# Attention of a one-core kernel with two accumulator banks and four score banks instead of one and five, values ahead of scores on TensorE, and its first loads in parts and in another order

## The reference, cut to what matters

```python
def chunk_mask(qpos, kpos):
    return (kpos // CHUNK)[None, :] <= (qpos // CHUNK)[:, None]          # CHUNK = 64

def mla_block_attend(qn, qp, kn, kp, v, qpos, kpos):
    s = jnp.einsum('bqhd,bkhd->bhqk', qn, kn) + jnp.einsum('bqhr,bkr->bhqk', qp, kp)
    s = jnp.where(chunk_mask(qpos, kpos), s.astype(F32) * MLA_SCALE, NEG_INF)
    p = jax.nn.softmax(s, axis=-1).astype(v.dtype)
    return jnp.einsum('bhqk,bkhd->bqhd', p, v)

def mla_prompt(q_nope, q_pe, ckv, kpe, w_ukv, pos):
    kv = jnp.einsum('bsl,lhe->bshe', ckv, w_ukv)
    k_nope, v = kv[..., :MLA_NOPE], kv[..., MLA_NOPE:]
    ...      # query block i attends to keys 0 .. (i + 1) * 128
```

## Time and profile before

| what | us |
|---|---|
| median of 3 runs (lowest, highest) | 3573.41 (3569.66, 3576.82) |
| the profiled execution | 3574.15, of which its span 3572.2 |
| PE busy, weight loads | 3074.6 (86%), 2356.9 (66%) |
| DVE busy | 1547.0 (43%) |
| ACT busy | 1063.8 (30%) |
| `mixer` | 0 to 1497.7 |
| `attention` | 1497.7 to about 2253 |
| the other blocks | to 3572.2 |

### The profile page before, as it was taken

How to read it: one execution, slowest core, us unless ns; L and a number is a source line. 1 busy time by engine, 2 the same in 40 slices (tenths; PEclk the granted TensorE clock), 3 DMA queues, 4 the chain that set the end, 5 groups by cost and what they waited for, 6 DMA issues and landing times. The chain is left out here.

```text
span 3572.2 us, 78385 instructions
## 1 busy us (share of the span) xinstructions
PE 3074.6 (86%) x28855; PEld 2356.9 (66%) x28856; DVE 1547.0 (43%) x3462; ACT 1063.8 (30%) x2645; POOL 436.1 (12%) x716
## 2 busy tenths in 40 slices
PE   5999999999999998588898989699719999999980
PEld 5888888888888887455555555355417776776660
DVE  0455555555555556377686868232310000000007
ACT  1333333333333333143444434122102222222220
POOL 0000000000000000100000000011142232222220
PEclk9999999999999999699999999899859999999995
DMA  4000010000011110200000010433227897774336
GB/s 171 26 25 25 25 28 25 25 25 26 26 29 32 28 30 23 59 9 22 16 16 22 1 33 1 148 126 129 86 103 240 265 346 237 240 216 88 76 65 217
DMA packets 136050, 297.30 MB, mean 83 GB/s; under 512 B 29403, under 2 KB 87037, under 8 KB 121341
## 3 DMA queue, kind: packets, MB, share of 16 engines
q1 hardware_dynamic: 113629, 215.65, 17.8%
q0 software_dynamic: 19520, 67.15, 8.1%
q10 hardware_dynamic: 2592, 9.96, 0.7%
HBM read 208.19 MB, written 84.53 MB: 82 GB/s over the span
## 5 line engine op out<-in xcount | busy, mean ns | idle before, releaser
L700 PE MATMUL mx_bank<-mx_xT,mx_w_in 128*128 128x128 f32 x5168 | 648.7, 283 | 23.7 <-DMA mx_w_in<-in_w_in 23.2
L700 PEld LDWEIGHTS mx_bank<-mx_xT,mx_w_in 128*128 128x128 f32 x5168 | 607.4, 195 | 78.8 <-issue 69.6
L1396 PE MATMUL at_bank<-at_kT,at_qT 128*128 128x512 f32 (+5 forms) x656 | 296.5, 539 | 2.4 <-DVE at_vals L1520 2.4
L2184 DVE SCALAR_TENSOR_TENSOR ex_th<-ex_th,ex_bank 128x256 f32<-128x256 f32 x64 | 27.0, 422 | 580.6 <-ACT ex_th L2100 580.6
L1368 ACT ACTIVATE at_PQ<-at_bank,at_nms 128x512 f32<-128x512 f32 (+5 forms) x328 | 193.1, 596 | 278.4 <-DVE at_nms L1496 183.2
L2171 PE MATMUL ex_bank<-ex_wd,ex_hT 128*128 x512 | 234.4, 601 | 2.1 <-ACT ex_hT L2106 2.1
L2151 PE MATMUL ex_bank<-ex_wg,ex_xT 128*128 x1024 | 233.9, 382 | 1.5 <-SPq L2021 1.5
L2151 PEld LDWEIGHTS ex_bank<-ex_wg,ex_xT 128*128 128x128 f32 x1024 | 196.1, 192 | 55.5 <-issue 31.6
L2151 PE MATMUL ex_bank<-ex_wu,ex_xT 128*128 x1024 | 231.5, 379 | 0.0
L1427 PEld LDWEIGHTS at_bank<-at_PT,at_vals 128*64 128x64 f32 (+1 forms) x2208 | 119.3, 139 | 156.3 <-issue 82.4
L1539 DVE COPY at_PT<-at_bank 128x512 f32<-128x512 f32 (+3 forms) x328 | 196.8, 601 | 56.8 <-PE at_bank L1408 42.8
(11 more groups left out here) (315 smaller groups left out, 4892.4 us busy)
## 6 DMA issues: line engine op xcount, KB each, us to landing
ex_wg<-in_w_eg SPq DMA_DIRECT2D x32, 1024.0 KB
ex_wu<-in_w_eu SPq DMA_DIRECT2D x32, 1024.0 KB
ex_wd<-in_w_ed SPq DMA_DIRECT2D x32, 1024.0 KB
mx_x<-in_x SPq DMA_DIRECT2D x19, 512.0 KB, 4.5
ro_x<-in_x SPq DMA_DIRECT2D x17, 512.0 KB, 3.9
scr_hx<-ro_h SPq DMA_DIRECT2D x17, 512.0 KB, 2.7
scr_acc<-ro_ha SPq DMA_DIRECT2D x17, 512.0 KB, 3.0
co_r<-scr_acc SPq DMA_DIRECT2D x17, 512.0 KB, 3.7
```

Of the source, the lines that this page charges most:

```text
L700: ins = pe.matmul(dst, w_in[:, k, col:col + n], xT[:, k, :], start=(k == 0), stop=(k == KC - 1))
L1396: t.mark(pe.matmul(bank[n % SB][:, 0:wd], qT[h][keys(h), j * P:(j + 1) * P], kT[h][keys(h), k0 * P:k0 * P + wd], start=True, stop=True), f ...
```

## The change

Three things. **Banks:** `SB` goes from 5 to 4, so scores use banks 0 to 3 and transposes 4 and 5; rows of even j accumulate their values in bank 6, odd ones in bank 7, each with its transposed reciprocals beside it. **Order and plan:** on PE a step is now values, `row_rec`, scores n + 4, transposes n; `row_rec` comes one step after the row's last values (`turned`), and ACT's copy and DVE's output with it; the first values of row j wait for output j - 2. The plan of value blocks comes out the same but for the last steps of a turn (84: three blocks instead of one; 86: none instead of two). **Loads:** SP first waits for PE's signal, which PE now gives after POOL's memsets alone; then it issues the weights, the prompt's latents in four parts, each with its own semaphore, and the rest. PE waits for a part before the K group that reads it, and for rotary keys and identity only before the first scores.

```diff
-    AHEAD, SB, TB = 4, 5, 2
+    AHEAD, SB, TB = 4, 4, 2
...
-        step = max(step, place[j, 1, g] + LAG, free)
+        step = max(step, place[j, 1, g] + LAG, free.get(j - 2, 0))
...
         if i + 1 == len(pairs) or pairs[i + 1][0] != j:
+            while step in row_end:
+                step += 1
+            if step not in share:
+                share[step] = 0
             row_end[step] = j
-            free = step + 2
+            turned[step + 1] = j
+            free[j] = step + 3
...
+        def summed(j):
+            return bank[6 + j % 2][:, 0:P]
+
+        def turned_sum(j):
+            return bank[6 + j % 2][:, P:2 * P]
...
-            sp.dma_start(lat[:, :, 0:n], lt[:, :, 0:n]).then_inc(latents.sem, 16)
...
+            def first_loads():
+                for k in range(4):
+                    cols = slice(512 * k, 512 * k + 512)
+                    sp.dma_start(lat[:, :, cols], lt[:, :, cols]).then_inc(lat_in[k], 16)
...
+                if isinstance(t.i, int):
+                    first_loads()
                 t.w0(ten, last_scores)
...
         def _(pe):
-            pe.wait_ge(latents.sem, latents.done(0))
             pe.wait_ge(setup, 6)
...
                         if gi == 0:
-                            if j > 0:
-                                t.w(vec, f"out_{j - 1}")
+                            if j > 1:
+                                t.w(vec, f"out_{j - 2}")
...
+                    pe.wait_ge(lat_in[n], 16 if n < 4 else 32)
                     for c in range(CKV):
...
+                pe.wait_ge(latents.sem, latents.done(0))
                 t.arrived(q_in)
...
                 for n in range(steps):
+                    for _ in range(share.get(n, 0)):
+                        next(v)
+                    if n in turned:
+                        row_rec(t, turned[n])
                     if n + AHEAD < count:
                         scores(t, n + AHEAD)
-                    for _ in range(share.get(n, 0)):
-                        next(v)
-                    if n in row_end:
-                        row_rec(t, row_end[n])
                     if n < count:
                         transposes(t, n)
```

More of the change, by code:

```diff
@@ L1196, in attention, with in_order @@
         if i + 1 == len(pairs) or pairs[i + 1][0] != j:
+            while step in row_end:
+                step += 1
+            if step not in share:
+                share[step] = 0
             row_end[step] = j
-            free = step + 2
-    steps = max(max(share) + 1, count)
+            turned[step + 1] = j
+            free[j] = step + 3
+    steps = max(max(share) + 2, count)
     last_use = {n: max(m for m in range(count) if m % NP == n % NP) for n in range(NP)}
-    def in_order(ahead, before, at, after):
+    def in_order(ahead, before, at, after, scores_last=False):
         names = [x for n in range(min(AHEAD, count)) for x in ahead(n)]
         for n in range(steps):
-            names += ahead(n + AHEAD) if n + AHEAD < count else []
-            names += before(n) + (at(n) if n < count else []) + after(n)
+            later = ahead(n + AHEAD) if n + AHEAD < count else []
+            names += before(n) + later if scores_last else later + before(n)
+            names += (at(n) if n < count else []) + after(n)
         return names
@@ L1217, in pv_names @@
                 out.append(f"PV{j}_{g}")
[L1218 removed]
+        return out + ([f"recT{turned[n]}"] if n in turned else [])
     def max_names(n):
@@ L1268, in attention @@
             ("tensor", ten_names), ("vector", vec_names), ("scalar", act_names), ("gpsimd", pol_names)))
-        latents = Dmas(nc, ctx, "at_latents", 10)
+        latents = Dmas(nc, ctx, "at_latents", 7)
+        lat_in = [ctx.enter_context(nc.semaphore(f"at_lat_in{k}")) for k in range(5)]
         setup = ctx.enter_context(nc.semaphore("at_setup"))
@@ L1380, in turn @@
                             t.w0(vec, last_out)
-                        t.mark(a.activation(recb[:], bank[7][:, P:2 * P], ACT.Copy), f"rec{j}")
+                        t.mark(a.activation(recb[:], turned_sum(j), ACT.Copy), f"rec{j}")
             engine_loop(a, act, turns, turn)
@@ L1426, in values @@
                             for h, m in ((0, m0), (1, m1)):
-                                ins = pe.matmul(bank[7][64 * h:64 * h + 64, 0:P], vals[0:rows, k0 + s, 64 * h:64 * h + 64],
+                                ins = pe.matmul(summed(j)[64 * h:64 * h + 64], vals[0:rows, k0 + s, 64 * h:64 * h + 64],
                                                 PT[0:rows, m % NPT, s, :], start=(gi == 0 and s == 0), stop=end)
@@ L1513, in output @@
                     t.left(o_out)
-                t.mark(v.tensor_tensor(o_sb[:, j, :], bank[7][:, 0:P], recb[:], ALU.mult), f"out_{j}")
+                t.mark(v.tensor_tensor(o_sb[:, j, :], summed(j), recb[:], ALU.mult), f"out_{j}")
             def turn(t):
```

36 lines of the change are left out of this document (18 added, 18 removed).

## The result

The changed kernel takes **3617.03 us** (median of 4 runs, 3614.94 to 3619.21) against 3574.53 (4 runs, 3569.66 to 3576.82): the ratio is **1.0118, interval 1.0106 to 1.013**, 42.5 us slower. The forecast was 3593.5 us, 19.4 us slower. The sign held and the time lies within the wide range of the prediction (3566 to 3620 us), but it is outside the forecast's own band (3583 to 3605 us), and the loss is more than twice the one forecast. The profiled execution took 3616.22 us with a span of 3614.1 us, 41.9 us more than the span before.

A forecast was written before the change was run, and what follows sets the result against it. PE and DVE were taken as close together, neither with slack for the other's waits. Heads +37.2, second accumulator -18.8, loads -5.8 and clock +6.8 made +19.4 us on 3574.15: 3593.5 us, band 3583 to 3605, range 3566 to 3620.

The forecast's parts named there:

- Heads: Four-chunk heads, rows 12 to 15: scores n+4 wait for exp n; seven loops a turn, +9.3 us a turn, +37.2 in all.
- Loop 64 to 68: Row 14's first head, end of exp 64 to end of exp 68: 9.30 us after the change, 8.06 before.
- 68 to 72: Row 14's second head, exp 68 to exp 72: 8.92 us after the change, 7.51 before.
- the heads are cheap: Rival: DVE's waits for transposes at heads take in most delay, 0.35 us a loop left; 3559 us, faster, chance 0.15.
- The clock: PE idle at the new heads drops the clock at some: one full price a turn, +6.8 us, bounds 0 and +24.
- clock at many heads: Rival: the clock falls at half of the heads or more, +24 instead of +6.8; 3611 us, chance 0.15.
- Second accumulator: Values of row j no longer wait for output j-1: -4.7 us a turn, -18.8 us, bounds -8 and -24.
- the count said no loss: Rows 8 to 11, three chunks a head: maximum n+4 can start 2.07 us after the scaled maximum, within 2.2 us.
- Loads: Weights first, latents in quarters: first matmul at 1507.5 instead of 1513.35 us, -5.8 us once, bounds -3 and -7.
- No change: Rival: about 0.9 us a loop at the heads and no fall of the clock; 3574 us, chance 0.13.
- faster: Rival case that heads are cheap, below 0.88 us a loop: 3559 us, chance 0.15.
- Not as it says: Rival: split loads queue behind one another, first matmul where it was; 3599 us, chance 0.07 with the rest as forecast.

## Why the prediction was right in sign and wrong in size

**Heads: right.** +9.3 us a turn forecast, +9.7 measured without falls of the clock (38.9 us instead of 37.2). Loop 64 to 68 read 9.69 (9.30 forecast), 68 to 72 8.71 (8.92). That it is the bank is shown by the kernel with four banks, which loses more there, and by the one with five and two accumulators, which has 57.0 us for chunks 48 to 76 instead of 64.35. The worked loop was short by 0.4 us, in the time from scores to transposes. The rival "the heads are cheap", on DVE's waits for transposes, falls: the copies did come to idle 30.0 us instead of 56.8, but the maximum that comes late stands ahead of the copy, as the text said against it.

**The clock: the step that failed.** The idle time was about right (PE waits 1.1 to 2.2 us at a head, and 1.61 to 2.23 where a fall followed; forecast 1.7 to 2.4), and so was the price: 17.4 us for 12 falls is 1.45 us each, against 1.7. The number of falls was wrong: the term took one full price a turn, +6.8 us, without a reason for just one, and there were 12 falls instead of 4, +17.4 us. I had gone by two waits, 1.98 us with a fall and 1.52 without, as if the length decided. The rows of after show that it doesn't. In turns two and three PE has nearly the same waits; here are three of each (timeline, PE), and below the clock of the 4 us behind each:

```profile
1818.11 1.12 PE L1416 MATMUL at_bank<-at_kT,at_qT 128*128 128x512 f32 x2 [2.23 <-ACT at_PQ L1389]
...
1828.90 1.62 PE L1416 MATMUL at_bank<-at_kT,at_qT 96*128 96x512 f32 x2 [1.61 <-ACT at_PQ L1389]
...
1838.83 1.12 PE L1416 MATMUL at_bank<-at_kT,at_qT 128*128 128x512 f32 x2 [1.73 <-ACT at_PQ L1389]
...
2014.81 1.12 PE L1416 MATMUL at_bank<-at_kT,at_qT 128*128 128x512 f32 x2 [2.22 <-ACT at_PQ L1389]
...
2032.46 1.12 PE L1416 MATMUL at_bank<-at_kT,at_qT 128*128 128x512 f32 x2 [1.93 <-ACT at_PQ L1389]
...
2050.52 1.38 PE L1416 MATMUL at_bank<-at_kT,at_qT 128*128 128x512 f32 x2 [1.91 <-ACT at_PQ L1389]
```

```profile
1819.00:1823.00 4.00, 4.00 (x20) 2.46 (x19) 1.38 (x2) 1.09 (x6) 0.00 (x0) 0.57 0.00 0
1829.00:1833.00 4.00, 4.00 (x10) 2.00 (x11) 1.38 (x2) 2.05 (x9) 0.00 (x0) 0.57 0.02 6
1839.00:1843.00 4.00, 4.00 (x31) 2.44 (x33) 2.08 (x3) 1.92 (x8) 0.00 (x0) 1.00 0.00 0
2015.00:2019.00 4.00, 4.00 (x32) 2.44 (x33) 2.08 (x3) 1.79 (x8) 0.00 (x0) 1.00 0.00 0
2033.00:2037.00 4.00, 4.00 (x36) 2.56 (x34) 2.31 (x5) 1.55 (x7) 0.00 (x0) 1.00 0.00 0
2051.00:2055.00 4.00, 4.00 (x20) 2.52 (x19) 1.38 (x2) 1.71 (x8) 0.00 (x0) 0.57 0.00 0
```

A wait of 2.23 us was followed by 0.57 in turn two, one of 2.22 by 1.00 in turn three; 1.61 by a fall, 1.93 by none, 1.91 by one again. So a single wait of 1.6 to 2.2 us may or may not cost 1.45 us, 12 times in 28 heads here (chunks 48 to 72 of four turns). What decides is not shown. The share could not be read from the trace before; with bounds of 0 and 24 us, all that it gave, a centre near the middle was the fairer term. The rival "clock at many heads" (half of the heads or more, +24 us in place of +6.8, 3611 us) came closest to the measured time and to the 12 falls. Behind it stood the Trainium skill, "TensorE: Matmul & The Clock Gate", "A second HAM failure mode: psum-queue depth-cycling", where short idle times between matmul groups make the clock go back and forth. The trace agrees, with 12 falls at scattered heads; I had given it too small a chance because one wait of 1.52 us passed.

**Second accumulator: mis-sized, 12.6 us instead of 18.8.** The first values of row 7 gave 2.4 us a turn instead of 3.0, and 1.6 of them are the fall of the clock behind that wait (12.86 us with it and 11.23 without, as the trace of the loads shows). Chunks 0 to 24 gave 1.6 as forecast (1.5). But rows 9 to 11, where the count said no loss, lost 0.8 us a turn, and the end lost 0.1 us instead of winning 0.2. The waits for the output were not all gone either: 7.9 us are left on the page, in turn two 1.7 us in two waits. That the 1.5 us came out was luck: chunks 4 to 8 gained 2.8 us and 12 to 16 2.4 us while 8 to 12 and 20 to 24 lost 2.1 and 1.2 us; the forecast had none of these four and their sum happened to be small.

**Loads: right in size,** -5.7 us by themselves and -5.1 us in the trace for -5.8 forecast, though the first matmul stands at 1509.95 and not at 1507.5: 1.7 us of that are the late start of the block, the rest the first quarter of the latents, which took 4.2 us from its issue instead of 3.5.

**The sum.** +37.2 - 18.8 - 5.8 + 6.8 against +38.9 - 12.6 - 4.7 + 17.4 (the loads at the first scores) and +2.5 in the gaps between turns, which the forecast left out. Of the 22.5 us missing in the spans the clock has 10.6, the accumulator 6.2, the gaps 2.5, and the rest is in small terms. The clock is not what makes the gaps longer: it is low around them for 6.8, 6.8 and 3.4 us, and was for 6.8 us at each before. PE waits 3.9 to 4.1 us ahead of the next turn's first key matmul instead of 3.0 to 3.3, and from the last output to that matmul it is 3.0 to 3.4 us in all five kernels with two accumulators, 2.2 to 2.7 in the others without unused matmuls at the end. Which step of the change does it stays open.

**The other rivals.** No change and faster wanted 0.9 us a loop or less; it was 1.39. "Not as it says" falls with the first matmul, which did come earlier.

**What the text said would show it.** It held, near enough, for the loop (9.69 us for 9.3), for the waits at the scores, and for the clock 53 us after a turn's first scores, which no longer falls. It did not hold for the first matmul (1509.95 us for 1507.5) or for the waits for `at_o_sb`, of which some are left. Rows 12 to 15 became longer by 13.6 us in turn two, not 9: that is where the falls were to be seen.

## What to carry to other kernels

Eight banks are a budget: a bank given to one use is to be priced at the place where its old use had been late last. Here a look-ahead bank was worth 68 us, a second accumulator with the new order some 13. The first question before taking a bank for a wait is whether the wait goes away by moving its work one step: here that gave 4.6 us without a bank to pay for, where the accumulator's gain was less than its bank cost. Where PE newly idles 1 to 2 us at a repeated place, count every one of these places as one that may lose the clock, and try one unused matmul in that time: the loops here were no longer with it than the ones without falls.

## What the runs showed of the hardware

- One unused matmul of 512 columns, 0.85 to 1.1 us in a wait of 1.1 to 2.2 us, kept the granted clock at 1.00 in chunks 48 to 76 of all four turns; without it 12 heads were followed by a fall to 1.2 GHz. It was worth 16.8 us of 3617.
- Two waits of PE alike to 0.01 us, at the same place of two turns and behind the same work (2.23 and 2.22 us), had different clocks behind them, 0.57 and 1.00. The same program lost 3, 3, 1 and 5 times in its four turns. A count from one turn, multiplied by four, can't see that. In the kernel with the loads alone the same wait of 1.98 us was followed by a fall in three turns and by none in the fourth, and the difference was 1.6 us.
- With five banks for scores and one for transposes, to put the scores behind the values cost 48 us; with four and two it saved 20. The same order had opposite signs with two bank plans.
